# The pooling branch's small matmuls are taken out of attention and put into the first column of the gate stage

## The chip, the cores and the metric

One Trainium2 chip, all 8 cores of it. The kernel is one program that runs on every core; each core computes one of the 8 sequences of the batch, with no traffic between the cores. The metric is the device time of the slowest core in microseconds (us). Five engines work side by side in a core: TensorE (PE, matrix products), VectorE (DVE), ScalarE (ACT), GpSimd (POOL, here only for the issue of the weight loads) and SyncE (SP, the other transfers). Each takes its own instructions strictly in the order in which they were written down.

## The reference

Two layers. In each, a token mixer (block-sparse attention beside a pooling branch, both gated) and then a gated MLP. What the change touches is the pooling branch and the merge:

```
proj = h @ w_in[layer]                                     # (B,S,IN_WIDTH)
q, k, v, u, gates = jnp.split(proj, splits, axis=-1)
y_a = moba_attention(q, k, v) @ w_branch_a[layer]
y_b = multiscale_pool(u, w_pool[layer], pool_scale[layer]) @ w_branch_b[layer]
g = jax.nn.sigmoid(gates)                                  # two gates, 1024 wide each
merged = g[:, :, 0] * y_a + g[:, :, 1] * y_b

def multiscale_pool(u, w_pool, pool_scale):                # 4 groups of 128 channels, windows 2, 4, 8, 16
    mixed = (window_sum / count[None, :, :, None] - uf).astype(u.dtype)
    y = jnp.einsum('bsgc,gcd->bsgd', mixed, w_pool).reshape(B, S, POOL_WIDTH)
    return y * pool_scale
```

The sequence has 2048 tokens, the model width is 1024; attention has 8 heads of 64.

## The kernel before

**Layout.** Activations lie transposed: 128 channels on the partitions, tokens along the free axis, in 4 chunks `c` of 512 tokens. A matmul takes a 128x128 block of weights and 512 tokens. The results land in the 8 banks of PSUM (`ps`), each of 128x512 float32 values, from which ScalarE or VectorE must take them before the bank can be written again.

**Attention.** `mixer` runs 160 steps `s` (4 pairs of heads `m`, 4 chunks of queries, 2 heads, and pieces of keys). A step has the scores of the step that follows (`scores`, L829 and L833, into banks 0 to 3), the exponential of its own scores on ScalarE (`attend`, L885, out `Pt`) and its values product (`values`, L902, into bank 4 or 5). Banks 6 and 7 serve all the rest in turn: the projections q, k, v and u, cut into four pieces each by `pieces` (L551, L585), which a planner, `m1_schedule`, deals out over the steps; the matmuls of the block gating (L721, L770); the transposes of finished attention (L924). `long_bank` hands a projection its bank; `short_bank` hands the other one to a small product that wants it in between. `later` puts a follow-up on a list with a step at which it is due, `run_due` works it off.

**The pooling branch.** Each of the 16 projections of u in a layer (4 groups `g` by 4 chunks `c`) is copied out of PSUM into `ub` (`u_done`: L657 on ScalarE, from step 120 on L655 on VectorE), summed by one to four additions on VectorE (L672, out `tA` and `tB`), and turned into mean minus token by `mixin` (L685, out `mx`). Six steps later `um` multiplies `mx` by the group's 128x128 matrix `wpl` (L698, one matmul of 512 columns, in a short bank) and ScalarE scales the result into `pooledT` (L700). There is one `mx`, so that each `mixin` has the preceding `um` issued first, and waits for it.

**The gate stage.** After the steps, what is left on the list is run, and then 8 columns `m` of output channels by 4 chunks `c`: two products of eight matmuls each for the two gates (`mm8`, L546, banks b0 and b0+1), four matmuls on `pooledT` (L968, bank b0+2), four on `attnT` (L971, bank b0+3), two sigmoids (L974, L976), and three operations on VectorE. b0 is 0 and 4 in turn.

**The order.** Everything is written in program order by hand; `Sched` only adds the waits that reads and writes of tiles and banks need.

## Time and profile before

| | |
|---|---|
| median of 3 runs | 1997.73 us (1995.74 to 2048.76) |
| the profiled execution | 1996.67 us |
| its span on the slowest core (core 3) | 1995.4 us |
| spans of the 8 cores | 1990.3 to 1995.4 us |
| PE busy | 1881.4 us, 94% |
| DVE busy | 1248.8 us, 63% |
| ACT busy | 833.1 us, 42% |
| steps of attention, layer 0 and layer 1 | about 98 to 325 us, 1043 to 1282.5 us |
| gate stages | 325 to 493.3 us, 1282.5 to 1449.9 us |

A time stands beside the span of its slowest core; what lies around the span is 1.3 us. In a row of the timeline the first number is the start in us from the span's start, the second the time until the end, then engine, line, operation, out<-in, shape and count; the bracket is the idle time of that engine before it and what ended it. The end of a matmul is modelled: a row of 0.38 us for one matmul of 512 columns says little, since the next one starts 0.216 us after it. Differences between starts are exact.

### The profile page before, as it was taken

To read this page: it belongs to the slowest core of one execution; us is meant where nothing else is said; L and a number is where in the kernel's file an instruction comes from. 1 tells how busy PE (TensorE), PEld (TensorE's weight loads), DVE (VectorE), ACT (ScalarE), POOL (GpSimd) and SP (SyncE) were. 2 spreads that over 40 slices of the span, in tenths; PEclk is the share of its full clock that TensorE was granted. 3 is DMA by queue.
4 is the path that set the end of the run, shared out by engine and by line. 5 is a ranking of instruction groups with operands and counts; after the bars stand their busy time and mean duration, and the time that the engine had idled before them with its cause. 6 is when DMAs were issued, how large, how long until landed. Compare 5 with 4: busy or idle time off the path is not lost.

```text
span 1995.4 us, 32572 instructions; the slowest of 8 cores (1990.3 to 1995.4 us)
## 1 busy us (share of the span) xinstructions
PE 1881.4 (94%) x12288; PEld 946.3 (47%) x12288; DVE 1248.8 (63%) x1712; ACT 833.1 (42%) x1018; POOL 124.9 (6%) x240
## 2 busy tenths in 40 slices
PE   3889998999999999999999998899999999999997
PEld 1545664444544444444456565444444444444443
DVE  1556554344688658768765557533457874885886
ACT  2467774222344224224446776522234430431442
POOL 1000000000000000000010000000001000000000
PEclk8889999999999999999999999999999999999998
DMA  9210111323133222222140002023214232233214
GB/s 201 54 17 12 18 18 17 43 32 48 17 48 43 37 38 39 38 41 34 21 58 10 12 2 44 12 38 43 32 17 59 37 43 37 36 40 43 31 18 169
DMA packets 38663, 79.61 MB, mean 40 GB/s; under 512 B 4320, under 2 KB 8544, under 8 KB 38496
## 3 DMA queue, kind: packets, MB, share of 16 engines
q0 software_dynamic: 33760, 60.39, 22.1%
q1 hardware_dynamic: 4752, 17.15, 2.5%
q8 instruction: 102, 1.67, 0.4%
q14 instruction: 49, 0.40, 0.1%
HBM read 129.51 MB, written 8.39 MB: 69 GB/s over the span
## 4 chain that ended last, share of the span: by engine, by line
PE 87%; DVE 5%; ACT 3%; issue 3%; DMA 2%; SPq 0%; DVEq 0%; POOL 0%; ACTq 0%; POOLq 0%
PE ps L546 41%; PE ps L1088 15%; PE ps L551 7%; PE ps L829 5%; PE ps L1027 5%; PE ps L902 3%; PE ps L971 3%; PE ps L968 3%; PE ps L585 2%; DVE hs L531 2%; DMA xs<-xt 1%; ACT Pt L885 1%; PE ps L520 1%; ACT pooledT L700 1%; PE ps L504 1%
## 5 line engine op out<-in xcount | busy, mean ns | idle before, releaser
L546 PE MATMUL ps<-hs,ring 128*128 128x512 bf16 x3776 | 831.6, 380 | 1.0 <-DVE xs L1012 1.0
L546 PEld LDWEIGHTS ps<-hs,ring 128*128 128x128 bf16 x3776 | 370.2, 98 | 449.2 <-issue 7.8
L885 ACT ACTIVATE Pt<-ps 128x1024 bf16<-128x1024 f32 x320 | 278.6, 894 | 101.9 <-PE ps L829 54.2
L1088 PE MATMUL ps<-hid,ring 128*128 128x512 bf16 x1408 | 306.8, 379 | 0.0
L1067 DVE SCALAR_TENSOR_TENSOR tg<-ps,pv,tg 128x1024 f32<-128x1024 f32 (+2 forms) x176 | 225.8, 1283 | 73.6 <-ACT tg L1063 62.7
L551 PE MATMUL ps<-hs,ring 128*128 128x512 bf16 x832 | 233.6, 392 | 18.5 <-ACT pooledT L700 7.4
L1063 ACT ACTIVATE tg<-ps,pv 128x1024 f32<-128x1024 f32 x88 | 106.1, 1206 | 328.5 <-PE ps L546 323.8
L1067 DVE SCALAR_TENSOR_TENSOR tv<-ps,pv,tv 128x1024 f32<-128x1024 f32 (+2 forms) x176 | 225.2, 1280 | 13.2 <-ACT tv L1063 4.0
L1088 PEld LDWEIGHTS ps<-hid,ring 128*128 128x128 bf16 x1408 | 137.2, 98 | 163.5 <-issue 0.6
L1063 ACT ACTIVATE tv<-ps,pv 128x1024 f32<-128x1024 f32 x88 | 106.1, 1205 | 196.6 <-PE ps L546 190.9
L829 PE MATMUL ps<-qz,kz 72*128 72x512 bf16 (+3 forms) x640 | 181.5, 354 | 1.1 <-DVE ksb L709 1.1
L978 DVE TENSOR_TENSOR s<-s,ps 128x512 f32<-128x512 f32 x64 | 44.0, 687 | 190.3 <-PE ps L968 190.3
L1108 DVE TENSOR_TENSOR xs<-xs,ps 128x512 f32<-128x512 f32 x128 | 86.5, 686 | 101.2 <-PE ps L1088 101.2
L493 ACT ACTIVATE sq<-xs 128x512 bf16<-128x512 f32 x128 | 79.1, 630 | 149.0 <-DVE xs L1012 148.5
L902 PEld LDWEIGHTS ps<-Vt,Pt 128*128 128x128 bf16 x2176 | 101.8, 98 | 72.4 <-issue 40.0
L902 PE MATMUL ps<-Vt,Pt 128*128 128x65 bf16 x2176 | 120.3, 195 | 13.8 <-ACT Pt L885 11.4
L551 PEld LDWEIGHTS ps<-hs,ring 128*128 128x128 bf16 x832 | 75.7, 99 | 106.7 <-issue 45.0
L974 ACT ACTIVATE s<-ps 128x512 f32<-128x512 f32 x64 | 38.2, 598 | 183.9 <-PE ps L546 180.9
L1012 DVE TENSOR_TENSOR xs<-xs,ps 128x512 f32<-128x512 f32 x128 | 83.3, 683 | 49.7 <-PE ps L1027 34.6
L1027 PE MATMUL ps<-mergedT,ring 128*128 128x512 bf16 x512 | 112.8, 379 | 0.0
L1078 DVE TENSOR_TENSOR hid<-tg,tv 128x1024 bf16<-128x1024 f32 x88 | 106.9, 1215 | 0.6
L1074 ACT ACTIVATE tg<-tg 128x1024 f32<-128x1024 f32 x88 | 92.1, 1047 | 0.0
(87 smaller groups left out, 1429.8 us busy)
## 6 DMA issues: line engine op xcount, KB each, us to landing
ring<-w_up POOLq DMA_DIRECT2D x88, 256.0 KB, 4.3
ring<-w_in POOLq DMA_DIRECT2D x64, 256.0 KB, 5.4
xs<-xt SPq DMA_DIRECT2D x16, 512.0 KB, 15.5
yt<-yst SPq DMA_DIRECT2D x16, 512.0 KB, 2.7
ring<-w_down POOLq DMA_DIRECT2D x32, 224.0 KB, 4.0
ring<-w_ab POOLq DMA_DIRECT2D x16, 256.0 KB, 5.3
ring<-w_out POOLq DMA_DIRECT2D x16, 256.0 KB, 4.9
ring<-w_down POOLq DMA_DIRECT2D x16, 256.0 KB, 4.2
```

What stands on the lines that cost most here:

```text
L546: S.op("pe", lambda e: [e.matmul(bank(b), w[:, kc, :], hs[:, c, kc, :], start=(kc == 0), stop=(kc == 7)) for kc in range(8)][-1], reads=[r ...
L551: S.op("pe", lambda e: [e.matmul(bank(b), w[:, kc, :], hs[:, c, kc, :], start=(kc == 0), stop=(kc == 7)) for kc in range(lo, hi)][-1], rea ...
L829: ins = e.matmul(ps[:, a:a + n], kz[0:72, st, h, kt * 128:(kt + 1) * 128], qz[0:72, h, c * 512 + qo:c * 512 + qo + n], start=True, stop=no ...
L885: S.op("act", lambda e: e.activation(Pt[:, pi, 0:n], ps[:, sl * 1024:sl * 1024 + n], AF.Exp, scale=0.125), reads=[PB[2 * sl], PB[2 * sl + ...
L902: ins = e.matmul(bank(ob, j * 128, j * 128 + 65), Pt[:, pi, a:a + 128], Vt[:, st, kt, h, :], start=new, stop=end, skip_group_check=True)
L1027: S.op("pe", lambda e: [e.matmul(bank(b), w[:, kc, :], mergedT[:, kc, c * 512:(c + 1) * 512], start=(kc == 0), stop=(kc == 7)) for kc in r ...
L1063: S.op("act", lambda e: e.activation(t, ps[:, p0:p0 + 1024], AF.Identity, bias=cbias, scale=c2), reads=here + [R_pv], writes=[rt[hf]])
L1067: S.op("dve", lambda e: e.scalar_tensor_tensor(t[:, lo:], ps[:, p0 + lo - d:p0 + 1024 - d], cc, t[:, lo:], ALU.mult, ALU.add), reads=back ...
L1074: S.op("act", lambda e: e.activation(tg[:, hf, :], tg[:, hf, :], AF.Silu), reads=[R_tg[hf]], writes=[R_tg[hf]])
L1078: S.op("dve", lambda e: e.tensor_tensor(hid[:, il, hf * 1024:(hf + 1) * 1024], tg[:, hf, :], tv[:, hf, :], ALU.mult), reads=[R_tg[hf], R_t ...
L1088: S.op("pe", lambda e: [e.matmul(bank(b), w[:, kc, :], hid[:, kc, c * 512:(c + 1) * 512], start=(kc == 0), stop=(kc == nk - 1)) for kc in ...
L1108: S.op("dve", lambda e: e.tensor_tensor(xs[:, c, m, :], xs[:, c, m, :], bank(b), ALU.add), reads=[R_x[c][m], PB[b]], writes=[R_x[c][m]])
```

## The change

`mixin` writes mean minus token straight into `pooledT`; `mx`, `um` and its place on the list are gone. The products with `wpl` are done in the gate stage's first column: per chunk, groups 0 and 1 ahead of the first gate product, groups 2 and 3 ahead of the second, in banks b0+2 and b0+3, each scaled back in place into `pooledT` by ScalarE. In all 8 columns the product on `attnT` now stands ahead of the one on `pooledT`, and VectorE's multiplications are swapped accordingly.

```
                 def mixin():
-                    run_due("um")
-                    S.op("dve", lambda e: e.scalar_tensor_tensor(mx[:, :], src[:, 16:528], 1.0 / WINS[g],
+                    dst = pooledT[:, g, c * 512:(c + 1) * 512]
+                    S.op("dve", lambda e: e.scalar_tensor_tensor(dst, src[:, 16:528], 1.0 / WINS[g],
                                                                   ub[:, i, 16:528], ALU.mult, ALU.subtract),
-                         reads=[rsrc, R_u[i]], writes=[R_mx])
+                         reads=[rsrc, R_u[i]], writes=[R_pool[g][c]])
...
-                    later(6, "um", True, um)
-
-                def um():
-                    b2 = short_bank()
-                    S.op("pe", lambda e: e.matmul(bank(b2), wpl[:, l, g, :], mx[:, :], start=True, stop=True),
-                         reads=[R_wpl, R_mx], writes=[PB[b2]])
-                    S.op("act", lambda e: e.activation(pooledT[:, g, c * 512:(c + 1) * 512], bank(b2), AF.Copy,
-                                                       scale=pv[:, pb + PV_PSC + g:pb + PV_PSC + g + 1]),
-                         reads=[PB[b2], R_pv], writes=[R_pool[g][c]])
...
+            def pool_mix(c, gs, b):
+
+                cs = slice(c * 512, (c + 1) * 512)
+                for k, g in enumerate(gs):
+                    S.op("pe", lambda e: e.matmul(bank(b + k), wpl[:, l, g, :], pooledT[:, g, cs], start=True, stop=True),
+                         reads=[R_wpl, R_pool[g][c]], writes=[PB[b + k]])
+                    S.op("act", lambda e: e.activation(pooledT[:, g, cs], bank(b + k), AF.Copy,
+                                                       scale=pv[:, pb + PV_PSC + g:pb + PV_PSC + g + 1]),
+                         reads=[PB[b + k], R_pv], writes=[R_pool[g][c]])
...
+                    if m == 0:
+                        pool_mix(c, (0, 1), b0 + 2)
                     mm8(b0, tiles[0][0], tiles[0][1], c)
+                    if m == 0:
+                        pool_mix(c, (2, 3), b0 + 2)
                     mm8(b0 + 1, tiles[1][0], tiles[1][1], c)
```

How the instructions stand at two places of layer 0. First PE at the end of the steps and the start of the gate stage; `wpl` marks the pooling matmuls, `atok` the last transposes, `hs,ring_56` the first gate product. Before:

```order
L551 MATMUL ps<-hs,ring_55 128x512 x2
L698 MATMUL ps<-mx,wpl 128x512
L902 MATMUL ps<-Vt,Pt 128x65 x8
L551 MATMUL ps<-hs,ring_55 128x512 x2
L902 MATMUL ps<-Vt,Pt 128x65 x2
L698 MATMUL ps<-mx,wpl 128x512
L924 MATMUL ps<-cbs,atok 128x128 x4
L698 MATMUL ps<-mx,wpl 128x512
L546 MATMUL ps<-hs,ring_56 128x512 x8
L546 MATMUL ps<-hs,ring_57 128x512 x8
```

and of the change:

```order
L551 MATMUL ps<-hs,ring_55 128x512 x2
L893 MATMUL ps<-Vt,Pt 128x65 x8
L551 MATMUL ps<-hs,ring_55 128x512 x2
L893 MATMUL ps<-Vt,Pt 128x65 x2
L915 MATMUL ps<-cbs,atok 128x128 x4
L954 MATMUL ps<-pooledT,wpl 128x512 x2
L546 MATMUL ps<-hs,ring_56 128x512 x8
L954 MATMUL ps<-pooledT,wpl 128x512 x2
L546 MATMUL ps<-hs,ring_57 128x512 x8
L974 MATMUL ps<-attnT,ring_58 128x512 x4
L977 MATMUL ps<-pooledT,ring_58 128x512 x4
```

The three pooling matmuls around the last values products and transposes are gone, and two pairs stand in each of the first four rounds of the gate stage.

Second ACT over the last steps of layer 0; `Pt` is the exponential, `s_83` and `s_84` the two sigmoids. Before:

```order
L885 ACTIVATE Pt<-ps 128x1024
L700 ACTIVATE pooledT<-ps,pv 128x512
L885 ACTIVATE Pt<-ps 128x1024 x3
L700 ACTIVATE pooledT<-ps,pv 128x512
L885 ACTIVATE Pt<-ps 128x1024 x3
L700 ACTIVATE pooledT<-ps,pv 128x512
L885 ACTIVATE Pt<-ps 128x256
L700 ACTIVATE pooledT<-ps,pv 128x512 x2
L974 ACTIVATE s_83<-ps 128x512
```

and of the change:

```order
L876 ACTIVATE Pt<-ps 128x256
L876 ACTIVATE Pt<-ps 128x1024 x7
L876 ACTIVATE Pt<-ps 128x256
L956 ACTIVATE pooledT<-ps,pv 128x512 x4
L980 ACTIVATE s_83<-ps 128x512
L982 ACTIVATE s_84<-ps 128x512
```

Between two exponentials ACT no longer has an instruction that waits for a pooling matmul; four of them stand ahead of each of the first four pairs of sigmoids. VectorE's order over the steps is the same but for one place early in layer 0, where a copy of `attnT` now stands three operations earlier and a copy of `qz` three later.

## Rows read from the trace of the kernel before

**Rows 1.** Spans and granted clock, the slowest core.

```profile
core 3: 1995.4 us, clock 0.979
```

**Rows 2.** Windows: attention and gate stage, both layers; busy us (count) by engine, PEclk, DMA share, GB/s.

```profile
98.00:325.05 227.05, 202.38 (x2257) 121.42 (x2258) 131.40 (x297) 161.32 (x204) 6.05 (x12) 0.97 0.13 18
325.05:493.30 168.25, 168.25 (x769) 75.74 (x768) 64.63 (x94) 40.21 (x66) 12.13 (x23) 0.99 0.25 34
1043.00:1282.54 239.54, 214.72 (x2425) 131.13 (x2422) 142.48 (x317) 161.35 (x203) 7.40 (x14) 0.97 0.13 19
1282.54:1449.90 167.36, 167.36 (x769) 75.49 (x768) 64.65 (x94) 40.10 (x66) 12.14 (x23) 0.99 0.25 35
```

**Rows 3.** Waits in attention of layer 0: us in total, times, longest.

```profile
PE ps L902 <- ACT Pt L885: 8.0, 16, 2.4
...
DVE mx L685 <- PE ps L698: 6.3, 5, 2.1
...
PE ps L551 <- ACT pooledT L700: 3.0, 7, 0.9
```

**Rows 4.** Timeline, layer 0, around one pooling matmul late in attention.

```profile
313.47 1.03 PE L551 MATMUL ps<-hs,ring 128*128 128x512 bf16 x4
314.34 0.38 PE L698 MATMUL ps<-mx,wpl 128*128 128x512 bf16 x1
...
314.81 0.69 ACT L700 ACTIVATE pooledT<-ps,pv 128x512 bf16<-128x512 f32 x1 [1.17 <-PE ps L698]
...
315.40 1.93 ACT L885 ACTIVATE Pt<-ps 128x1024 bf16<-128x1024 f32 x2
...
315.65 0.59 PE L551 MATMUL ps<-hs,ring 128*128 128x512 bf16 x2 [0.25 <-ACT pooledT L700]
...
316.56 0.41 PE L902 MATMUL ps<-Vt,Pt 128*128 128x65 bf16 x8 [0.32 <-ACT Pt L885]
```

**Rows 5.** Timeline, layer 0: the first values product that waits behind a pooling evacuation.

```profile
142.21 0.22 PE L902 MATMUL ps<-Vt,Pt 128*128 128x65 bf16 x2 [0.17 <-ACT Pt L885]
```

**Rows 6.** Timeline, layer 1: first and last of three pooling matmuls that wait for a bank.

```profile
1109.90 0.38 PE L698 MATMUL ps<-mx,wpl 128*128 128x512 bf16 x1 [0.95 <-DVE attnT L927]
...
1174.56 0.38 PE L698 MATMUL ps<-mx,wpl 128*128 128x512 bf16 x1 [0.96 <-DVE ksum L573]
```

**Rows 7.** Waits in attention of layer 1.

```profile
PE ps L551 <- ACT pooledT L700: 4.5, 10, 0.9
```

**Rows 8.** Windows, layer 1, 1224 to 1260 us.

```profile
1224.00:1260.00 36.00, 28.60 (x269) 14.50 (x267) 29.25 (x62) 21.69 (x27) 1.06 (x2) 1.00 0.19 31
```

**Rows 9.** Timeline, layer 1, DVE's sums in that stretch, one after another.

```profile
1239.39 0.71 DVE L672 TENSOR_TENSOR tA<-ub 128x527 f32<-128x527 f32 x1
1240.21 0.71 DVE L672 TENSOR_TENSOR tB<-tA 128x525 f32<-128x525 f32 x1
```

**Rows 10.** Timeline, the end of attention in both layers.

```profile
320.28 0.22 PE L902 MATMUL ps<-Vt,Pt 128*128 128x65 bf16 x2 [0.52 <-ACT Pt L885]
...
320.89 0.42 DVE L912 TENSOR_TENSOR atok<-ps,rec 128x256 bf16<-128x256 f32 x1
...
324.46 0.59 PE L698 MATMUL ps<-mx,wpl 128*128 128x512 bf16 x1 [2.37 <-DVE mx L685]
...
1276.48 0.23 PE L902 MATMUL ps<-Vt,Pt 128*128 128x65 bf16 x2
...
1276.75 0.69 DVE L685 SCALAR_TENSOR_TENSOR mx<-tA,ub 128x512 bf16<-128x512 f32 x1 [1.43 <-PE ps L902]
```

**Rows 11.** Timeline, the first rounds of the gate stage: both gate products.

```profile
324.84 6.16 PE L546 MATMUL ps<-hs,ring 128*128 128x512 bf16 x16
...
328.54 1.28 ACT L974 ACT_TABLE_LOAD   x1 [2.71 <-PE ps L546]
...
332.56 3.62 PE L546 MATMUL ps<-hs,ring 128*128 128x512 bf16 x16
...
1282.33 5.29 PE L546 MATMUL ps<-hs,ring 128*128 128x512 bf16 x16
```

More of the change, by code:

```diff
@@ L970, in mixer @@
                          reads=[rab] + [R_pool[g][c] for g in range(4)], writes=[PB[b0 + 2]])
-                    S.op("pe", lambda e: [e.matmul(bank(b0 + 3), wab[:, kc, :], attnT[:, kc, cs],
-                                                   start=(kc == 0), stop=(kc == 3)) for kc in range(4)][-1],
-                         reads=[rab] + [R_attn[g][c] for g in range(4)], writes=[PB[b0 + 3]])
                     S.op("act", lambda e: e.activation(s0[:, ti, :], bank(b0), AF.Sigmoid),
```

11 lines of the change are left out of this document (7 added, 4 removed).

## The prediction

> **What bounds the kernel now.** I read the table of cores first: the slowest core's clock is 0.979 of full speed over the span [rows 1], the cores agree, so one core may stand for all. Then the windows by stage [rows 2]. The gate stages are TensorE's alone: busy for the whole of 168.25 and 167.36 us, and with 768 matmuls that is 0.216 us each once the slow start is set aside (below). Nothing but fewer columns or a faster clock shortens them, and each matmul put there costs its 0.216 us. Attention is different: PE is busy 202.4 of 227.05 us and 214.7 of 239.5 us, so some 25 us in each layer are holes. No other engine is full over the whole stage (VectorE 131 and 142 us, ScalarE 161 and 161 us). Holes there come from engines that wait for each other, and are what the change can win.
>
> The list of waits says who opens them. In layer 0 PE waits 7 times, 3.0 us, for the pooling evacuation L700, and 16 times, 8.0 us, for an exponential [rows 3]. The timeline shows that half of the second kind are the first kind in disguise [rows 4]. The pooling matmul starts at 314.34. ScalarE has been idle for 1.17 us ahead of the evacuation at 314.81: the evacuation stands in its queue ahead of an exponential whose scores were in PSUM more than a microsecond before, and it cannot start until the matmul has run, which PE reaches only after four projection matmuls (313.47). The exponential starts at 315.40 in place of about 313.8. PE then waits twice, for the bank (until 315.65) and for the late exponential (until 316.56).
>
> **What each part costs.** The sums are made against the profiled execution, 1996.67 us; the median is 1.1 us above it, and I shift the result by that.
>
> *The holes, layer 0.* Sixteen pooling matmuls go. Fourteen stand in the steps and two in the tail. Waits for L700 ahead of L551: 3.0 us [rows 3]. Of the 16 waits for exponentials, eight come directly behind a pooling evacuation, from 0.17 us [rows 5] to 0.52 us [rows 10], together 3.0 us. A printed idle time is too short by 0.17 us, because a matmul's end is modelled late: in [rows 4] four matmuls from 313.47 and the pooling matmul end by pace at 314.56, and in the same way the last piece ahead of 315.65 ends 0.42 us before it where 0.25 is printed. For 15 waits that adds 2.5 us. With the 14 matmuls' own 0.216 us, 3.0 us, the sum is 11.5 us. I take 10.5, since at one place (about 131 us) a wait for a q evacuation on ScalarE stands right behind and only moves up. Bounds: 6 us, if half of the waits are replaced by waits for the next exponential or for VectorE, and 13 us, if the steps that follow also run closer together.
>
> *Layer 1 up to 1224 us.* Three pooling matmuls, each of which waits 0.95 or 0.96 us for a bank that VectorE is still reading [rows 6]. Without them PE has other work in the queue, and the next user of that bank comes steps later. 3 x (0.96 + 0.17 + 0.216) is 4.0 us, and two of the waits for L700 [rows 7], 0.2 and 0.25 us, behind them, with the 0.17 each, 0.8 us: 4.8, taken as 5.0 with a little of what follows; bounds 3 and 6.5.
>
> *Layer 1 from 1224 to 1260 us.* Seven pooling matmuls, and most of the 4.5 us that PE waits for L700 in this layer [rows 7]. But here VectorE is the engine behind: busy 29.25 of 36 us [rows 8], and its sums depend on each other, one starting 0.81 us after the other though it is 0.71 long [rows 9], so that the 62 instructions fill the stretch but for 2.6 us of waiting for other engines. The copy out of a u bank stands in VectorE's queue behind the sums of the preceding u, and this order is not changed. What is taken from PE here is waited for at the next copy. I take 1.3 us, half of VectorE's idle time; bounds 0 and 5.
>
> *Layer 1 from 1260 us.* Four pooling matmuls, 0.86 us, with two more of those waits, 0.25 us each, one of 0.32 us for an exponential as in [rows 4], and 0.17 us for each, 1.3 us: 2.2 us; bounds 1.2 and 2.6.
>
> *The tail.* This is the surest part. In layer 0 the last values product starts at 320.28, and before the gate stage may start at 324.84 [rows 11], PE has a pooling matmul, the transposes, which need the bank of the one before, and a last pooling matmul, which waits 2.37 us for VectorE's sum [rows 10]. After the change only the transposes are left. They need `atok`, which VectorE starts 0.61 us after the values product and ends at 321.31; 0.15 us later (the gap between an evacuation's end and the matmul behind it, 315.50 to 315.65 in [rows 4]) they run for 0.22 us, and the gate stage starts at 321.7: 3.1 us earlier. In layer 1 the values product is at 1276.48, and `mixin` at 1276.75 stands in VectorE's way [rows 10], which waited for a pooling matmul and no longer does. By the same steps, 1276.48 + 0.61 + 0.42 + 0.15 + 0.22 is 1277.9 where 1282.33 stands now: 4.4 us. Together 7.5 us. VectorE's sum for the last u is still to be done, but its product is now in the fourth round, 18 us later: that work is the cover, and it costs nothing.
>
> *The clock.* In the first round of the gate stage the sixteen gate matmuls take 6.16 us in layer 0 and 5.29 in layer 1, in the second 3.62 [rows 11]: TensorE runs at 1.2 GHz in place of 2.4 for a while, after the holes of the tail. With 1.2 us of hole left instead of about 4.5, less than it has had elsewhere in attention at full clock, I expect it not to fall. That gives 2.5 and 1.7 us, 4.1 with rounding; bounds 0 and 4.2.
>
> *The gate stage.* 32 matmuls by 0.216 us, 6.9 us, all on the path. Does more come on top? A round starts with two pooling matmuls (0.43 us). By [rows 4] ScalarE starts 0.47 us after the first one's start, the second evacuation starts 0.59 us later, takes 0.69, and PE goes on 0.15 us behind: 1.90 us after the start. The next pair writes the same banks at 0.43 + 1.73 = 2.16 and 2.38 us. The second pair's last evacuation ends for PE at 4.06, and the product on `attnT` wants that bank at 4.32. Covered by the second gate product, with 0.26 us to spare; the product on `pooledT` comes 0.86 us later still, which is what the swap is for. ScalarE has six operations of 0.6 us or little more in a round of 6.05 us, and the 1.28 us table load of the first sigmoid [rows 11] fits once. VectorE has in a round what it had before. If the cover is gone, each round loses up to 1.1 us for every evacuation (below). No transfer is moved: the queues of GpSimd and SyncE hold the same instructions in the same order, and the weights of the first three columns are loaded steps ahead.
>
> The Trainium skill, page "ScalarE: Activation LUTs", section "Table sets: the hidden batching unit", says that copies are in every table set. This bears on copies that now stand between sigmoids; the trace shows copies between exponentials without a load, and none yet between sigmoids. Were it otherwise, two loads a round would come on top, and ScalarE would have 6.2 us of work in a round of 6.05: some microseconds in all, inside the range.
>
> **The sum.** 10.5 + 5.0 + 1.3 + 2.2 + 7.5 + 4.1 - 6.9 = 23.7 us. From the median, 1997.7 - 23.7 = 1974.0 us.
>
> **Rivals.**
> *VectorE and the exponentials take it back.* What happens from 1224 to 1260 us happens wherever u is projected, and the clock falls in the tail all the same: 5 + 3 + 0 + 1 + 7.5 + 0 - 6.9 is 9.6 us, 1988 us. For it speaks [rows 8], against it that in layer 0 VectorE itself waits 6.3 us for pooling matmuls [rows 3], time that it gets back.
> *More comes free.* The upper bounds: 13 + 6.5 + 5 + 2.6 + 7.5 + 4.2 - 6.9 is 31.9 us, 1966 us. For it speaks that VectorE, too, was held by `mixin` waiting on PE.
> *The work is only moved.* TensorE has as many matmuls as before, and if the holes are set by the loop from scores to exponential to values and not by the pooling instructions in it, they open elsewhere: the 32 matmuls cost 6.9 us here or there, and the time stays at 1997.7. Against it speak [rows 4], where the blocked exponential can be seen, and the tail. The Trainium skill, page "Perfetto Trace Analysis", section "Identifying the Most-Contended Engine", sends the reader to the engine with most work in it, TensorE here, whose work the change leaves as it is; by that rule alone there is no gain. I give it little, because the holes are in the trace.
> *Slower.* The evacuations in the gate stage are not covered. One exposed evacuation costs PE 1.09 us (314.34 to 315.65 less 0.216, [rows 4]); 32 of them 35 us, which turns the gain into 2009 us. It decides from 3.0 us lost per round in the eight rounds, and would need ScalarE to be late by more than a gate product's 1.73 us in each. Only a spare time of 0.26 us stands against it at the tightest place, but missing that by a little costs tenths, not microseconds.
>
> **How the numbers follow.** Forecast 0.66, VectorE takes it back 0.14, more comes free 0.10, only moved 0.07, slower 0.03. The range runs from 1963 to 1985 us: it holds the forecast, most of the better case and part of the way to the worse. Two per cent, about what a measurement of this kernel can tell from no change, is 40 us; no case reaches that, and I give 0.04 to faster and 0.01 to slower, with 0.95 between.
>
> **What would show it right or wrong.** In the profile after: attention of layer 0 some 13 to 14 us shorter and of layer 1 some 12 to 13 us (tails included), with VectorE's waits for the pooling matmul gone; the gate stages together 2.8 us longer (6.9 less the clock's 4.1); the first sixteen gate matmuls at 0.216 us each. A gate stage longer by more than 7 us together would show uncovered evacuations; PE waiting for `ub` or `ksum` in place of `pooledT` would show VectorE taking over. The sum is wrong first in the two attention terms, where I argue from waits one at a time and the engines answer together.

## The result, and the profile after

The changed kernel takes 1976.67 us, the median of four runs (1976.08 to 1977.64); the kernel before has 1997.73. Ratios and intervals, here and below, leave out executions in which the cores of a die ran at a lower granted clock for long (the kernel before took up to 2334 us then). The ratio of runs on the same chip is 0.990, with a 95% interval of 0.9876 to 0.9924, which is 20 us. The time is 2.7 us above the forecast of 1974.0 us and inside its range, and within 2% of the kernel before. The prediction's sum is 23.7 us, and 21.1 us came between the two medians. This section reads where they came from; the runs behind it say why.

The table of cores of the changed kernel, two of its rows:

```profile
core 0: 1969.6 us, clock 0.984
...
core 2: 1976.6 us, clock 0.981
```

The clock is what it was [rows 1]. Core 2 is the slowest and is read from here on. The windows of its four stages, from the first matmul of each stage to the first of the next (columns as in [rows 2]; mixed over two layers they would hide the finding):

```profile
99.88:311.86 211.98, 194.07 (x2208) 119.87 (x2241) 128.82 (x291) 152.45 (x189) 5.80 (x11) 0.97 0.12 17
311.86:481.07 169.21, 168.42 (x772) 76.70 (x785) 66.67 (x99) 49.17 (x81) 12.13 (x23) 1.00 0.25 36
1031.35:1261.13 229.78, 209.60 (x2370) 131.70 (x2401) 140.33 (x313) 153.03 (x188) 7.40 (x14) 0.96 0.13 18
1261.13:1430.34 169.21, 168.37 (x771) 76.72 (x785) 66.69 (x99) 49.16 (x81) 12.13 (x23) 1.00 0.25 36
```

The windows of [rows 2] were cut a few tenths of a microsecond differently. Cut in the same way as here, from first matmul to first matmul, core 3 of the kernel before has 226.54, 168.30, 239.10 and 167.44 us. So attention is shorter by 14.56 us in layer 0 and by 9.32 us in layer 1, and the gate stages are longer by 0.91 and 1.77 us: 21.2 us in all. The spans differ by 18.8 us, since three things outside these stages go the other way by 2.4 us together: core 2's attention starts 1.6 us later (99.88 against 98.30, ahead of any changed instruction), the stretch between the layers takes 0.2 us more and the end 0.6 us more. Core 3 of the kernel before is also the one core with a longer layer 1 than the rest, 239.1 us against 237.6 on the other seven; by the medians over all eight cores, attention is shorter by 14.4 us in layer 0 and by 7.8 us in layer 1.

The waits in layer 0's attention (engine, line, releaser: total, times, longest):

```profile
PE ps L761 <- DVE qz L562: 5.5, 2, 4.7
...
PE ps L893 <- ACT Pt L876: 4.4, 7, 2.4
```

Line 893 is the values product, L902 in the kernel before, and 876 the exponential. Its 16 waits of 8.0 us [rows 3] are 7 of 4.4 us. The wait for a pooling evacuation and VectorE's wait for a pooling matmul have no row any more. The longest wait for an exponential is the same in both kernels, 2.4 us, and so is the one for `qz`: the start of attention isn't touched.

The end of attention in layer 0, and the first two rounds of the gate stage:

```profile
310.45 0.23 PE L893 MATMUL ps<-Vt,Pt 128*128 128x65 bf16 x2
...
311.64 0.38 PE L915 MATMUL ps<-cbs,atok 128*128 128x128 bf16 x4 [0.96 <-DVE atok L903]
311.86 0.59 PE L954 MATMUL ps<-pooledT,wpl 128*128 128x512 bf16 x2
312.29 1.89 PE L546 MATMUL ps<-hs,ring 128*128 128x512 bf16 x8
312.33 1.26 ACT L956 ACTIVATE pooledT<-ps,pv 128x512 bf16<-128x512 f32 x2 [2.43 <-PE ps L954]
...
314.02 0.59 PE L954 MATMUL ps<-pooledT,wpl 128*128 128x512 bf16 x2
314.45 1.89 PE L546 MATMUL ps<-hs,ring 128*128 128x512 bf16 x8
...
315.77 1.28 ACT L980 ACT_TABLE_LOAD   x1
316.18 1.03 PE L974 MATMUL ps<-attnT,ring 128*128 128x512 bf16 x4
317.04 1.03 PE L977 MATMUL ps<-pooledT,ring 128*128 128x512 bf16 x4
...
317.90 0.59 PE L954 MATMUL ps<-pooledT,wpl 128*128 128x512 bf16 x2
```

From the last values product to the gate stage it is 1.41 us, where [rows 10, 11] have 320.28 to 324.84, 4.56 us: 3.15 us for a forecast of 3.1. Eight gate matmuls take 1.89 us, 7 x 0.216 and the last one's 0.38, from the first one on; in [rows 11] the first sixteen took 6.16. And the round is 28 matmuls long, 311.86 to 317.90, 6.04 us by 0.216: PE waits for neither pair of evacuations. ScalarE is done with the second ahead of the table load at 315.77, and PE reaches the product on `attnT`, which needs that bank, at 316.18. Both evacuations, 1.26 us, fit under eight matmuls.

Layer 1 is another matter. The stretch of [rows 8, 9] in the changed kernel, as windows and as timeline:

```profile
1236.00:1240.00 4.00, 3.53 (x30) 1.62 (x30) 3.48 (x9) 3.09 (x4) 0.00 (x0) 1.00 0.02 4
1240.00:1243.00 3.00, 1.06 (x14) 0.59 (x14) 2.69 (x6) 1.02 (x1) 0.53 (x1) 0.92 0.30 40
1243.00:1249.00 6.00, 5.94 (x36) 3.22 (x37) 2.79 (x5) 1.41 (x2) 0.00 (x0) 0.50 0.13 24
```

```profile
1239.19 0.68 DVE L655 COPY ub<-ps 128x512 f32<-128x512 f32 x1
...
1240.03 0.38 PE L915 MATMUL ps<-cbs,atok 128*128 128x128 bf16 x4 [0.44 <-DVE ub L655]
...
1240.26 0.71 DVE L672 TENSOR_TENSOR tA<-ub 128x527 f32<-128x527 f32 x1
...
1241.08 0.70 DVE L672 TENSOR_TENSOR tB<-tA 128x525 f32<-128x525 f32 x1
...
1241.88 0.69 DVE L685 SCALAR_TENSOR_TENSOR pooledT<-tB,ub 128x512 bf16<-128x512 f32 x1
1242.49 0.41 DVE L918 COPY attnT<-ps 128x512 bf16<-128x512 bf16 x1
...
1243.06 1.01 PE L551 MATMUL ps<-hs,ring 128*128 128x512 bf16 x2 [1.97 <-DVE attnT L918]
...
1245.48 1.91 PE L551 MATMUL ps<-hs,ring 128*128 128x512 bf16 x4
```

The transposes run at 1240.03, but VectorE copies their result out only at 1242.49: two sums and the difference, 0.7 us each, stand ahead of that copy in its queue. The bank comes free late, and PE has been idle for 1.97 us when the next projection starts. After that hole the matmuls are slow: four take 1.91 us in place of 1.03, and the granted clock from 1243 to 1249 us is 0.50, the lower level. VectorE is busy for 2.69 of the 3 us around the hole, and for 3.48 of the 4 us before it. Core 0 is the core with the shortest attention here, 225.91 us. It has the same longest waits, and one window of it shows what it doesn't have:

```profile
1236.00:1256.00 20.00, 16.72 (x174) 9.32 (x171) 15.56 (x32) 11.83 (x13) 0.91 (x2) 1.00 0.09 15
```

Its clock stays at 1.00 through the same hole of 1.97 us. From the 30th to the 31st of VectorE's 32 reciprocals (operations that both cores have) core 2 takes 14.4 us and core 0 takes 11.4. So 3.0 of the 3.9 us between the two cores are the slow matmuls behind this hole. The rest, 0.9 us, was nearly all there at the first reciprocal: core 2's clock was 0.50 until 1041 us, core 0's until 1038. All eight cores have the hole of 1.97 us; on six the clock fell behind it, on cores 0 and 6 it did not.

### The profile page after: what moved, and what is told of

Read it like the earlier page. It is cut to its first block, busy times and chain, and to the rows that moved or that the text cites. A ratio compares the mean times of both kernels' runs of the same rounds, so it can differ in the third digit from the quotient of the medians.

```text
span 1976.6 us, 32462 instructions; the slowest of 8 cores (1969.6 to 1976.6 us)
## 1 busy us (share of the span) xinstructions
PE 1862.3 (94%) x12076; PEld 946.8 (48%) x12288; DVE 1248.5 (63%) x1712; ACT 833.5 (42%) x1018; POOL 124.9 (6%) x240
## 4 chain that ended last, share of the span: by engine, by line
PE 87%; DVE 5%; issue 3%; ACT 3%; DMA 2%; SPq 0%; DVEq 0%; POOL 0%; ACTq 0%; POOLq 0%
PE ps L546 41%; PE ps L1094 15%; PE ps L551 7%; PE ps L820 5%; PE ps L1033 5%; PE ps L893 3%; PE ps L974 3%; PE ps L977 3%; PE ps L585 2%; DMA xs<-xt 1%; DVE hs L531 1%; ACT Pt L876 1%; PE ps L520 1%; PE ps L504 1%; PE ps L824 1%
## 5 line engine op out<-in xcount | busy, mean ns | idle before, releaser
L546 PE MATMUL ps<-hs,ring 128*128 128x512 bf16 x3699 | 824.1, 379 | 5.0 <-DVE xs L1018 1.0
L551 PE MATMUL ps<-hs,ring 128*128 128x512 bf16 x753 | 218.7, 394 | 19.1 <-DVE hs L531 6.9
```

The source lines that it names most:

```text
L546: S.op("pe", lambda e: [e.matmul(bank(b), w[:, kc, :], hs[:, c, kc, :], start=(kc == 0), stop=(kc == 7)) for kc in range(8)][-1], reads=[r ...
L551: S.op("pe", lambda e: [e.matmul(bank(b), w[:, kc, :], hs[:, c, kc, :], start=(kc == 0), stop=(kc == 7)) for kc in range(lo, hi)][-1], rea ...
```

## The experiments

Twelve runs were made. The granted clock has to be told first. In the two series with e1 to e7 and the repeat of the changed kernel, most cores had 0.81 of full clock from about 72 to 233 us, but for some stretches at 0.50 up to 138 us, whatever the kernel, and layer 0's attention is 9 to 10 us longer on those cores. In the series with e9 to e12 no core had it. So the kernels are compared by stage, between cores of the same clock. The table has the median over the cores in us; stages run from first matmul to first matmul as above. A dash: no core of that kind.

| kernel | attention, layer 0, full clock | same, 0.81 | attention, layer 1 (all cores) | gate stages |
|---|---|---|---|---|
| before | 226.4 | - | 237.6 (237.6 to 239.1) | 168.1, 168.1 |
| changed | 211.9 | - | 229.8 (225.9 to 231.4) | 169.2, 169.2 |
| changed, again | 212.1 | 221.1 | 227.8 (225.8 to 228.7) | 169.2, 169.2 |
| e1 swap only | 226.3 | 236.4 | 238.2 (236.3 to 239.8) | 167.3, 167.3 |
| e2 no product | - | 221.1 | 227.7 (227.2 to 229.8) | 165.8, 165.8 |
| e4 late evacuation | 224.1 | 234.1 | 237.0 (237.0 to 237.1) | 167.4, 168.1 |
| e5 in place | - | 236.5 | 244.8 (243.7 to 245.2) | 167.4, 167.3 |
| e6 uncovered | 211.9 | 222.3 | 228.5 (225.8 to 228.7) | 184.4, 183.6 |
| e7 u on ScalarE | - | 221.6 | 220.6 (220.5 to 222.1) | 169.2, 169.2 |
| e9 in place, same order | 226.8 | - | 237.3 (237.1 to 238.8) | 168.0, 167.7 |
| e10 before, u on ScalarE | 227.3 | - | 239.8 (236.4 to 239.8) | 168.2, 167.1 |
| e11 both on ScalarE | 220.8 | - | 225.1 (224.4 to 226.5) | 169.2, 169.2 |
| e12 matmul kept | 216.5 | - | 232.7 (232.5 to 234.2) | 170.4, 169.2 |

**The swap alone.** The kernel before, with the two products of a gate round and their two multiplications in the order of the change:

```
+                    S.op("pe", ... bank(b0 + 3) ... attnT ...)
                     S.op("pe", ... bank(b0 + 2) ... pooledT ...)
-                    S.op("pe", ... bank(b0 + 3) ... attnT ...)
...
+                    S.op("dve", ... s0 ... bank(b0 + 3) ...)
                     S.op("dve", ... s1 ... bank(b0 + 2) ...)
-                    S.op("dve", ... s0 ... bank(b0 + 3) ...)
```

> The kernel before with only the gate stage's swap: the product on attnT ahead of the one on pooledT, VectorE's multiplications swapped with them. The pooling matmuls stay in attention. My theory is that the swap has nothing to do with the gain: 1996 to 1998 us. The rival, that VectorE or ScalarE were late for the pooled product in the gate stage of before, would have part of the 21 us here: 1985 to 1994 us.

Ratio 1.0019 (0.9966 to 1.0071), the gate stages as in the kernel before. The swap does nothing by itself.

**The product left out.** The changed kernel without the 32 pooling matmuls and their evacuations. It leaves the pooled group's matrix and its scale out, so that the gate stage reads plain differences:

```
-                    if m == 0:
-                        pool_mix(c, (0, 1), b0 + 2)
...
-                    if m == 0:
-                        pool_mix(c, (2, 3), b0 + 2)
```

> The changed kernel without the product with the pooling matrices and without pool_scale: pooledT keeps mean minus token, and the gate stage has neither the 32 matmuls nor their 32 evacuations. Its time against the changed kernel's 1976.7 us is the price of the product in its new place. My theory, everything covered: 32 x 0.216 is 6.9 us, so 1969.8 us. If evacuations are exposed (rival), the product costs more and this kernel comes out below 1967 us.

The gate stages take 165.76 us on every core, 3.45 us less than the 169.21 of the changed kernel, which is 16 x 0.216. Attention is that of the changed kernel. So the moved work costs its matmuls' 6.9 us, and nothing comes on top. By whole times it is about the same: 1980 us here, on a chip where most cores had 0.81, and 1986 to 1987 us for the changed kernel on another such chip.

**The tail alone.** The kernel before, with only the last two pooling products of each layer taken out of attention and into the rounds of their own column groups:

```
+                    if last2:
+                        ... pooledT[:, g, c * 512:(c + 1) * 512] ...
+                        return
...
+                    if m == 0 and c >= 2:
+                        S.op("pe", ... pooledT[:, 0, cs] ...)
+                        S.op("act", ... pooledT[:, 0, cs] ...)
```

> The kernel before, but of the 16 pooling products of a layer only the last two (group 0, chunks 2 and 3, the ones behind the last values product) go to the gate stage, in rounds 3 and 4 of its first column; the other 14 stay in attention with mx. Isolates the tail. My theory: 7.5 us of waits in the two tails, and 4.1 us of clock in the first round of the gate stages: 1997.7 - 11.6 is 1986 us. If the clock falls all the same, 1990 us. If the tail was not on the path, 1997 us.

1996.29 us beside 2008.56 us of the kernel before in that series: 12.3 us by these medians, 10.6 us by the ratio of 0.9947 (0.9929 to 0.9966). By stages, attention and gate stage together (their border moves in this kernel) take 388.7 us in layer 0 on the two cores at full clock, 4.7 us less than in e1, and 399.5 us in layer 1, 6.0 us less. Two products of sixteen give half of the change's time. The forecast for them was 7.5 us of tail and 4.1 us of clock.

**The evacuation put off a step.** The kernel before, with the evacuation recorded one step after its matmul, so that an exponential goes ahead of it:

```
-                    S.op("act", lambda e: e.activation(pooledT[...], bank(b2), AF.Copy, ...
+                    later(1, "ev%d" % b2, False, lambda: S.op(
+                        "act", lambda e: e.activation(pooledT[...], bank(b2), AF.Copy, ...
```

> The kernel before with the pooling matmul where it was, but its evacuation on ScalarE put on the list for the next step, as the projections' evacuations are, so that it stands behind the next exponential in ScalarE's queue. If the exponential held up behind the evacuation is what opens the holes (my theory for layer 0), some 4 to 8 us go: 1990 to 1994 us, with ScalarE's wait for the pooling matmul gone. If the bank is what holds PE, its wait for the evacuation ahead of the projections grows by as much as is won: 1996 to 1999 us.

Ratio 0.9959 (0.9918 to 1.0), an interval that reaches from no gain to more than I expected. By stages it is less than the 4 to 8 us of my theory: 2.2 us in layer 0 (2.3 at 0.81) and 0.6 us in layer 1 against the kernel before, 1.1 against e1. The waits in layer 0 on a core at full clock:

```profile
PE ps L551 <- ACT pooledT L701: 5.8, 9, 1.4
...
PE ps L903 <- ACT Pt L886: 5.3, 8, 2.4
```

The waits for exponentials fall (5.3 us against 8.0 in [rows 3]), as they should if half of them were evacuations in disguise. But PE then waits longer for the bank, 5.8 us against 3.0. The order mostly chooses which of the two comes late; the larger gain needs the evacuation to leave.

**The changed kernel again**, without an edit, in the series of e5, e6 and e7.

> The changed kernel once more, as the line that the other three runs are read against. Both theories expect a ratio to the kernel before of 0.985 to 0.993. If its cores are granted the full clock only from about 230 us on, as most cores of the last chip were, the theory of holes expects less than 21 us of gain in layer 0: at 0.81 of the clock the matmuls are longer, and the holes that the change takes out are partly filled already. The gate stages should again take 169.2 us each.

1986.2 and 1986.9 us, ratio 0.9862 (0.9733 to 0.999). My second expectation fell: on cores at 0.81 the attention of layer 0 is 221.1 us against 236.4 of e1, 15.3 us less, no smaller a gain than the 14.2 at full clock (226.3 to 212.1).

**In place.** The kernel before, with VectorE's difference written straight into `pooledT`, the matmul reading it there, and no call that forces the pending matmul ahead of the next difference:

```
-                    run_due("um")
-                    S.op("dve", lambda e: e.scalar_tensor_tensor(mx[:, :], ...
+                    dst = pooledT[:, g, c * 512:(c + 1) * 512]
+                    S.op("dve", lambda e: e.scalar_tensor_tensor(dst, ...
...
-                    S.op("pe", lambda e: e.matmul(bank(b2), wpl[:, l, g, :], mx[:, :], ...
+                    S.op("pe", lambda e: e.matmul(bank(b2), wpl[:, l, g, :], pooledT[...], ...
```

> The kernel before with one thing changed: the difference (sum less sub-sums) is written by VectorE straight into pooledT, the pooling matmul reads it there, and ScalarE evacuates over it. VectorE then no longer waits for the pooling matmul that last read mx (6.3 us over 5 waits in layer 0, 3.0 and 2.4 us at the two such rows that I read). The matmuls, their evacuations and the wait of TensorE's in-order queue on pooledT stay where they were. If my steps are right and both kinds of wait count, this brings the part of VectorE alone: 2 to 5 us, that is about 1993 to 1996 us where the kernel before has 1997.7, a ratio of 0.9975 to 0.999. If the wait on mx was the root of all the holes (the matmul was late because VectorE was late), it brings nearly all that the change brings outside the tails: 9 to 12 us, ratio about 0.995. If the holes come from the matmul's place in TensorE's queue alone, nothing: 1.000.

None of the three came: it is slower, ratio 1.007 (1.0008 to 1.0132). Layer 0 stands still, and layer 1 loses 6.6 us against e1. Without the forced call the pooling matmuls stand later in PE's queue, most by two or three steps, and one of them now asked for a bank whose u VectorE had not copied out yet, since three sums and the difference stood ahead of that copy. From the timeline of layer 1:

```profile
1250.88 0.69 DVE L685 SCALAR_TENSOR_TENSOR pooledT<-tA,ub 128x512 bf16<-128x512 f32 x1
1251.49 0.69 DVE L655 COPY ub<-ps 128x512 f32<-128x512 f32 x1
...
1252.32 0.38 PE L698 MATMUL ps<-pooledT,wpl 128*128 128x512 bf16 x1 [3.31 <-DVE ub L655]
```

PE waits 3.31 us here. The run mixed two things, a wait taken away and an order changed, and can't price the first.

**In place, in the old order.** The same with `run_due("um")` left in. Every engine's instructions then stand in the order of the kernel before:

```
                     run_due("um")
-                    S.op("dve", lambda e: e.scalar_tensor_tensor(mx[:, :], ...
+                    dst = pooledT[:, g, c * 512:(c + 1) * 512]
+                    S.op("dve", lambda e: e.scalar_tensor_tensor(dst, ...
```

> The kernel before with VectorE's difference written straight into pooledT and the pooling matmul reading it there, as in the run in place, but with every instruction left in the order of the kernel before on every engine (the run in place had moved the pooling matmuls a step later, and lost 5 to 6 us in layer 1 between two reciprocals of the VectorE-bound stretch). So this one takes away VectorE's wait for the pooling matmul and nothing else. The run in place gained nothing in layer 0 nor in the first 200 us of layer 1, so I now expect nothing: attention within 1 us of the kernel before in both layers, ratio 0.999 to 1.001. If the wait on mx is worth what I had put beside it, attention is 2 to 5 us shorter over both layers, ratio 0.9975 to 0.999.

Ratio 0.9999 (0.9989 to 1.0009). VectorE's wait for the pooling matmul, 6.3 us in [rows 3], is worth nothing by itself: nothing that sets the time was waiting for VectorE there.

**The matmul kept in attention.** The changed kernel, with each pooling matmul issued a second time at its old place, into a bank that nobody reads, and without an evacuation:

```
                 def mixin():
+                    run_due("um")
...
+                    later(6, "um", True, um)
+
+                def um():
+                    b2 = short_bank()
+                    S.op("pe", ... bank(b2), wpl[:, l, g, :], pooledT[...] ...)
```

> The changed kernel with the 32 pooling matmuls done twice: once in the gate stage as changed, and once in the attention stage at their old places, into a bank that nobody reads. Every other instruction of the attention stages stands as in the kernel before on every engine, without the evacuations. It splits what left attention into matmul and evacuation. If the evacuations cost the time (32 of 0.66 us on ScalarE, ahead of exponentials, and banks 6 and 7 given back late), it keeps most of the gain: 0 to 8 us above the changed kernel. If the matmul's wait in TensorE's queue on VectorE's difference costs it, most of the gain outside the tails goes: 10 to 15 us above the changed kernel. My prediction had the waits on the evacuations ahead (3.0 us of 7 in layer 0 and 4.5 of 10 in layer 1 by name, and the 2.5 us behind each matmul), so I expect 4 to 9 us above the changed kernel, the matmuls' own 6.9 us mostly in holes.

1984.67 us beside 1996.04, ratio 0.9944 (0.9927 to 0.9961). In layer 0 attention is 216.5 us: without the sixteen evacuations 9.9 of the 14.5 us are won, and the matmuls hold the other 4.6. Of these, 2.9 us are the tail: from the last values product to the gate stage it is 4.32 us here (309.87 to 314.19), where the changed kernel has 1.41, since the last pooling matmul still waits:

```profile
309.87 0.23 PE L901 MATMUL ps<-Vt,Pt 128*128 128x65 bf16 x2
...
313.81 0.59 PE L699 MATMUL ps<-pooledT,wpl 128*128 128x512 bf16 x1 [2.37 <-DVE pooledT L686]
```

The other fourteen matmuls cost 1.7 us together, 0.12 us each, little more than half of their own 0.216 us: about half of their time stood in holes. In layer 1 the evacuations are worth 4.9 us and the matmuls 2.9 of the 7.8 us that the medians differ by. The median is 8.0 us above the changed kernel's 1976.67 us, taken in another series: inside the 4 to 9 us of the theory of evacuations, at its upper end.

**Uncovered evacuations.** The changed kernel, with all four pooling matmuls of a round behind the gate matmuls, right ahead of the products that need them:

```
-                    if m == 0:
-                        pool_mix(c, (0, 1), b0 + 2)
                     mm8(b0, tiles[0][0], tiles[0][1], c)
-                    if m == 0:
-                        pool_mix(c, (2, 3), b0 + 2)
                     mm8(b0 + 1, tiles[1][0], tiles[1][1], c)
+                    if m == 0:
+                        pool_mix(c, (0, 1), b0 + 2)
+                        pool_mix(c, (2, 3), b0 + 2)
```

> The changed kernel with one thing changed: in the first round of the gate stage all four pooling matmuls of a column group stand behind the sixteen gate matmuls, right ahead of the attention and pooled products, so that nothing covers their evacuations. An evacuation took 0.63 us of ScalarE; the second pair of matmuls waits for the banks of the first pair (about 1.3 to 1.5 us), the attention product for the last evacuation's bank (the same again): 2.5 to 3 us in each of the 8 rounds, 20 to 24 us in all if the cover was what made the change cheap: about 1997 to 2001 us, the whole gain gone, and more if the clock falls in those gaps. The rival, that ScalarE keeps up and the cover is not needed (the matmuls of the next round would take up the slack), expects under 5 us, 1977 to 1982 us.

The gate stages take 184.4 and 183.6 us, together 29.6 us more than covered; the ratio to the kernel before is 1.0014 (0.9977 to 1.0051). The whole gain is gone. The first round of core 0:

```profile
308.61 3.62 PE L546 MATMUL ps<-hs,ring 128*128 128x512 bf16 x16
...
312.06 0.59 PE L954 MATMUL ps<-pooledT,wpl 128*128 128x512 bf16 x2
312.54 2.57 ACT L956 ACTIVATE pooledT<-ps,pv 128x512 bf16<-128x512 f32 x4 [5.88 <-PE ps L954]
313.37 0.38 PE L954 MATMUL ps<-pooledT,wpl 128*128 128x512 bf16 x1 [0.71 <-ACT pooledT L956]
313.95 0.38 PE L954 MATMUL ps<-pooledT,wpl 128*128 128x512 bf16 x1 [0.20 <-ACT pooledT L956]
...
315.25 1.02 PE L973 MATMUL ps<-attnT,ring 128*128 128x512 bf16 x4 [0.93 <-ACT pooledT L956]
...
316.98 3.62 PE L546 MATMUL ps<-hs,ring 128*128 128x512 bf16 x16
```

A round is 8.37 us (308.61 to 316.98) where the covered one has 6.04: 2.33 us for each of eight rounds is 18.6 us, near my 20 to 24. The other 11 us are the clock, which falls in these gaps on most cores; in this core's layer 1 (178.5 us, the clock at 1.00) the stage is 9.3 us longer, four times 2.33.

**The copies of u on ScalarE, in the changed kernel.** In the changed kernel, as in the one before, VectorE copies u out of PSUM in later steps, 13 of 16 in layer 1:

```
-                        late_u = now[0] >= 120
+                        late_u = False
```

> The changed kernel with one thing changed: the copies of the u projections out of PSUM stay on ScalarE throughout (in the changed kernel 13 of 16 in layer 1 are VectorE's, 0.69 us each). My account of why layer 1 gave 9.3 us and not 12.9 is that VectorE bounds it from about 1204 us on; then taking some 9 us of copies off VectorE there brings layer 1 forward by 2 to 5 us: 1972 to 1975 us. The rival, that ScalarE (153 of 230 us busy in layer 1's attention, and every score waits for it) sets the pace there, expects the same time or 2 to 6 us more.

1979.55 us (1978.83 to 1980.88), ratio 0.9829 (0.9736 to 0.9922), some 7 us under the changed kernel in the same series, more than the 2 to 5 us expected. All of it is in layer 1's attention: 220.6 us against 227.8. Its windows, on a core of this kernel and then on the same core of the changed kernel in that series:

```profile
1041.64:1262.18 220.54, 204.63 (x2403) 128.35 (x2401) 132.48 (x300) 159.44 (x201) 7.40 (x14) 0.99 0.13 19
...
1228.00:1244.00 16.00, 15.49 (x162) 8.75 (x161) 13.88 (x29) 13.17 (x17) 0.53 (x1) 1.00 0.12 19
1244.00:1260.00 16.00, 15.09 (x152) 8.51 (x151) 9.59 (x22) 13.01 (x17) 0.53 (x1) 1.00 0.12 17
```

```profile
1042.91:1270.75 227.84, 207.93 (x2404) 129.76 (x2402) 140.46 (x313) 152.99 (x188) 7.40 (x14) 0.98 0.12 18
...
1228.00:1244.00 16.00, 14.74 (x138) 8.32 (x139) 13.35 (x28) 8.74 (x10) 0.53 (x1) 0.89 0.12 17
1244.00:1260.00 16.00, 13.57 (x121) 7.09 (x119) 12.29 (x24) 7.86 (x9) 0.53 (x1) 0.89 0.11 18
```

8 us of copies have gone from VectorE (140.46 to 132.48) and 6.5 us have come to ScalarE. PE runs 162 and 152 matmuls in the two stretches of 16 us where it ran 138 and 121, and the clock no longer falls there. Much of the gain comes ahead of the hole: aligned by the reciprocals, some 4.5 us of the 7 are won between the 27th and the 30th, before PE waits 1.97 us in the changed kernel. In its series this kernel is the fastest.

**The same edit in the kernel before.**

```
-                        late_u = now[0] >= 120
+                        late_u = False
```

> The kernel before with the copies of the u projections left to ScalarE throughout, the same edit as in the run that made the changed kernel's layer-1 attention 5 to 9 us shorter. If VectorE bounds the later part of layer 1's attention in the kernel before too, this gains 2 to 4 us there (that stretch of 36 us has 2.6 us of VectorE idle, and ScalarE has the pooling evacuations besides), ratio 0.998 to 0.999; and the change, counted between this kernel and the changed kernel with the same edit, is worth 13 to 17 us in layer 1's attention. If the matmuls' holes bound it there, it gains nothing, and if ScalarE does, it loses 2 to 5 us.

Ratio 0.9993 (0.9983 to 1.0004). Layer 1 is 1.2 us shorter on three cores and 2.2 us longer on the other five (236.4 and 239.8 us against 237.6). While the pooling products are in the attention stage, this relief of VectorE, paid for by ScalarE, is worth nothing; with them gone, it is worth 7 us. Counted between the two kernels that have this edit, the change brings 19 us in layer 1 by the medians, and 16 from this kernel's best core to the other's: above the 12.9 us that I had forecast for it.

**Both copies on ScalarE.** The changed kernel with the edit of e7, and the copy of the transposed attention on ScalarE besides:

```
-                            S.op("dve", lambda e: e.tensor_copy(attnT[...], trb[:, 0:512]),
+                            S.op("act", lambda e: e.activation(attnT[...], trb[:, 0:512], AF.Copy),
```

> The changed kernel with the copies of the u projections on ScalarE throughout and the copies of the transposed attention (attnT, 0.42 us each on VectorE) there as well. ScalarE is busy some 153 us of 212 to 230 in each layer's attention, and a copy there stands behind an exponential of 1.02 us. If VectorE is still the later engine after the first edit, another 1 to 3 us; if ScalarE now is, 2 to 6 us more than with the first edit alone. I expect the second: 0 to 4 us above it, a ratio of 0.983 to 0.986 to the kernel before.

Ratio 0.9908 (0.9884 to 0.9932), above e7 by more than expected: 220.8 us in layer 0 against the changed kernel's 212, and 225.1 in layer 1 against 220.6. ScalarE is busy 162.49 and 164.69 us in these stages. Thirty-two more copies there stand in the way of exponentials, as the pooling evacuations did: about 9 us in layer 0 for sixteen of them, against 9.9 us for the sixteen evacuations. (The copies of u alone had cost 0.5 us in layer 0: 221.6 us in e7 against 221.1, at 0.81.)

## Why the prediction was right in the main, and the step that failed

The steps for layer 0, the tails and the gate stage held. The step that failed is layer 1's attention ahead of its tail. There the prediction lets three holes close for good, because "the next user of that bank comes steps later", and it puts the clock at nothing outside the first rounds of the gate stage. Its first two terms, 5.0 and 1.3 us, came out as 3.2 and -0.2 us on the slowest cores. What the runs showed in their place are waits for VectorE shortly behind each of the closed holes, and a fall of the clock worth 3.0 us behind one wait of 1.97 us. The terms one by one:

- *Holes of layer 0*: 10.5 forecast, 11.4 measured (14.56 less the tail). The mechanism was an evacuation on ScalarE ahead of an exponential and ahead of PE's bank. e12 shows it: 9.9 us of layer 0's gain goes with the evacuations alone. e4 shows that moving the evacuation doesn't do. Where I counted the fourteen matmuls' own 3.0 us in full, they had been half hidden; the waits on the evacuations were worth correspondingly more.
- *VectorE's wait for the pooling matmul* stood in the prediction as time that VectorE gets back. It is worth nothing (e9). It was no term of the sum, only an argument against a rival, and a bad one.
- *Tails*: 7.5 forecast. Layer 0 is 3.15 us by the rows above (3.1 forecast). Layer 1 goes from 5.85 us, 1276.48 to 1282.33 [rows 10, 11], to 1.41 us (the last values product is at 1259.72 and the gate stage at 1261.13), 4.4 us (4.4 forecast).
- *Clock in the first rounds*: 4.1 forecast (its two parts, 2.5 and 1.7, make 4.2). The stages of core 3 were 168.30 and 167.44 us where full clock gives 165.76 (e2): 4.2 us, all gained.
- *Gate stage*: 6.9 us forecast, and 3.45 us in each layer (e2 against the changed kernel). With the clock's 4.2 us set against it, the gate stages are 2.7 us longer together, 2.8 forecast. The cover holds, and was needed: 2.33 us a round without it (e6). I priced the rival "slower" at 1.09 us for each evacuation; e6 has 0.58 us, 2.33 by 4, and 0.9 us with the clock. With it the rival would have come out at 2000 to 2001 us (e6's ratio by 1997.7), not at 2009.
- *Layer 1 up to 1225 us of the kernel before*: 5.0 forecast, 3.2 measured, with the two kernels aligned by VectorE's 32 reciprocals. Half of the 3.2 us was not in my reckoning. Behind the second of the three holes the clock fell on core 3 alone, and cost it 1.7 us against core 0:

```profile
1122.00:1125.00 3.00, 3.00 (x19) 1.60 (x18) 0.79 (x4) 1.40 (x2) 0.00 (x0) 0.50 0.00 0
```

```profile
1122.00:1125.00 3.00, 3.00 (x39) 1.95 (x37) 1.76 (x4) 2.26 (x3) 0.00 (x0) 1.00 0.00 0
```

  The first row is core 3's, the second core 0's, both of the kernel before. The holes themselves gave 1.6 us for the 4.8 that I had counted: nothing at the first, 0.8 us at each of the other two. PE comes to the next waits sooner, and those are for VectorE. Of the changed kernel, core 2:

```profile
1100.82 0.34 PE L712 MATMUL ps<-ksb,qz 72*128 72x8 bf16 x8 [0.77 <-DVE qz L562]
...
1107.66 0.59 PE L551 MATMUL ps<-hs,ring 128*128 128x512 bf16 x2 [0.28 <-DVE ksum L573]
...
1110.29 0.38 PE L761 MATMUL ps<-cbs,btok 128*128 128x128 bf16 x4 [0.68 <-DVE rec L902]
...
1162.87 0.38 PE L761 MATMUL ps<-cbs,btok 128*128 128x128 bf16 x4 [0.68 <-DVE rec L902]
```

  The waits of 0.77 and 0.68 us are new.
- *Layer 1 from there to 1265 us*: 1.3 forecast, -0.2 measured (the gain is 3.2 us at 1224.76, 3.9 at 1251.85 and 3.1 at 1265.43). The prediction's sentence "what is taken from PE here is waited for at the next copy" is right as to who is waited for. But the waits come in one piece, 1.97 us, and behind it the clock fell, which cost core 2 another 3.0 us. On cores 0 and 6, where it did not fall, the same stretch gained 2.9 us against core 3 of the kernel before, more than forecast.
- *Layer 1 from there to the last values product*: 2.2 forecast, 1.8 measured. With the tail's 4.4 the four parts make the 9.3 us. e7 shows the cause: with VectorE relieved, the wait of 1.97 us and the slow stretch are both gone (the longest wait of PE from 1225 us on is 1.4 us), and some 7 us with them.
- *The likeliest rival* was right in kind for some 40 us of layer 1's attention, as its own row said [rows 8], and wrong for the rest. *Only moved* fell: the time is not set by the loop of scores, exponential and values alone.

The Trainium skill, page "Perfetto Trace Analysis", section "Identifying the Most-Contended Engine", sends the reader to the engine with the highest occupancy, TensorE here. The trace agrees that the time was to be won there: TensorE was busy for 94% of the span, and the 21 us came out of its holes and out of the slow matmuls behind them. What doesn't follow is the rival's reading, that with as many matmuls as before there is no gain. Most of the holes in layer 0 had been made by ScalarE's queue, with ScalarE busy 161 us of 227. The prediction's other question, whether copies between sigmoids load tables, is answered by the timeline: one load in the gate stage (315.77), as before.

The 7 us of e7 divide roughly so. Cores 4, 5 and 6 of the repeated changed kernel kept the full clock behind the hole and have 225.8 to 226.0 us in layer 1's attention; that is about 5.3 us above e7's 220.6, and the other 2 us are the clock of the cores on which it fell. What stays open is why, behind the same hole, it falls on some cores and not on others.

## What to carry to other kernels

An operation that two engines take turns at can cost more than its work. Ask, for each such operation, what stands behind it in the second engine's queue: here sixteen copies of 0.69 us held exponentials and a bank back, and their removal gave 9.9 us, while the fourteen matmuls outside the tail cost 1.7 us. Put such pairs where independent work of one engine covers the other's, and check the cover in microseconds: eight matmuls (1.73 us) for two evacuations (1.26 us).

An engine's wait is worth something only if somebody waits for that engine. VectorE's 6.3 us of waiting were worth nothing, and its relief was worth nothing in one kernel and 7 us in the next: after each change the next engine in line is to be looked up again, stage by stage.

## What the runs showed of the hardware

The clock can fall behind a small hole, and then the hole costs more than its length. In layer 1 of the changed kernel PE waited once for 1.97 us on core 2, having been busy for 3.53 of the 4 us up to 1240 us, and then ran at 0.50, 1.2 GHz, from 1243 to 1249 us: four 512-column matmuls took 1.91 us instead of 1.03. Then it was back at 2.4 GHz. All eight cores had this wait of 1.97 us; six fell, and cores 0 and 6 kept 1.00. In the kernel before, all eight had a wait of 0.96 us at about 1119 us, and the clock fell behind it on core 3 alone. So such a hole is a risk of a slow stretch, not its certain cause. Without the hole (e7) none of the eight cores fell from 1225 us to the end of attention, with waits of up to 1.4 us.

The clock was also granted at a value between the two levels. Two cores of e1, the same program on the same chip, as windows:

```profile
180.00:230.00 50.00, 49.63 (x535) 31.43 (x532) 23.66 (x54) 34.94 (x43) 0.53 (x1) 0.81 0.07 12
```

```profile
180.00:230.00 50.00, 47.17 (x602) 31.35 (x608) 24.92 (x59) 37.58 (x48) 1.58 (x3) 1.00 0.08 12
```

The first row is core 0's, the second core 4's. At 0.81 PE is nearer to full (49.63 of 50 us) and does less, 535 matmuls against 602. PE's idle time is smaller there, and yet the change gained as much: 15.3 us against 14.2. So a share of busy time tells little of what can be won unless the clock is read beside it. In the profiled executions it came in pairs of cores: in e1 all but 4 to 7, in e3 all but 6 and 7, in e4 and in the repeat of the changed kernel all but 2 and 3, in e6 all but 0 and 1, in e2, e5 and e7 none excepted. The Trainium skill, page "TensorE: Matmul & The Clock Gate", section "Seeing it yourself", knows a limiter that takes a whole die to 13/16 of the clock while several of its cores are dense, and holds it as long as that load lasts. The trace agrees on the level, 0.81. These traces disagree on the rest: cores 2 and 3 of a die had 1.00 while 0 and 1 had 0.81, and from 240 us to the end of the gate stage all had 1.00 but for falls to 0.50, under matmuls as dense (PE busy for the whole of the gate stage). Why it ended at about 233 us, and why it came in two of the four series alone, is open.
